# One-hot operands moved from ScalarE to VectorE, and a pacing term taken out, in a transformer block with retrieved experts

## The chip, the core and the metric

The kernel runs on one core of a Trainium2 chip. Its engines have queues of their own and meet only at semaphores: TensorE (PE: matmuls and transposes), VectorE (DVE), ScalarE (ACT), GpSimd (POOL, here only the issuer of gathers) and SyncE (SP, here only the issuer of weight loads). Everything is float32. The metric is the device time of one launch in microseconds; lower is better.

## What is computed

512 tokens of width 1024 go through two blocks. The first has three kinds of attention, one of them over compressed keys, and a gated feed-forward part. The second has a short convolution, a gated recurrence, and an expert layer. Two pieces matter here. The compressed keys are a small two-layer network over blocks of 32 tokens:

```python
blocks = kv[:, idx] + pe[None, None, :, None, :]
return jax.nn.gelu(flat @ w1) @ w2          # flat: 2048 wide, w1: 2048 x 256, w2: 256 x 64
```

And the expert layer picks, for each token and each of 8 heads, 16 of 16384 experts by a top-16 over pair sums, so 128 experts in all:

```python
expert = i1 * N_KEYS + i2                    # two indices of 0..127
u = jnp.take(u_tab, eb, axis=0)
a = gelu(einsum('td,thkd->thk', xb, u));  w = gates * a
vv = jnp.take(v_tab, eb, axis=0)
y = einsum('thk,thkd->td', w, vv)
```

## The kernel before

**Groups.** The 512 tokens are four tiles of 128 (t = 0 to 3), worked in two groups g of two tiles. Each group runs through project, attend, merge, mlp, mixer and queries. The expert layer of a group is a list of steps (`EXPERTS[g]`, written by `expert_steps`): `best`, `pairs`, `numbers` (the top-16 of one head), `job` (one gathered row per token, used by one VectorE instruction over 128 x 1024) and `spread` (below). POOL issues one gather of 512 KB per job, as early as the slot it goes to is free, which is when VectorE has done the job that used the slot before. There are 7 slots in group 0 and 12 in the first 128 jobs of group 1.

**Pacing.** The steps of group 0 are laid beside the dense work of group 1. TensorE's program decides where: `mm` adds the estimated time of each matmul to `state["spent"]`, and `take`, called for each PSUM bank, ticks off steps against it. The index reached is noted in `paced`, and VectorE and ScalarE run their steps up to that index (`catch_up`) before they touch that bank. TensorE executes no instruction for these steps, so its own order does not depend on them. At the start of attend in group 1, `settle` brings the list to a fixed step, the gate weights of tile 0, and sets `spent` to zero.

**compressed(g)** computes the hidden layer of the compression: four banks (`hid`, two for keys and two for values), each 16 matmuls, then the second layer (`kct`, `vcb`), which VectorE copies out of PSUM at L1198 and L1206. In group 1 all this stands ahead of `settle`. The first score of attend needs the copy `CQ` (L1312), which VectorE does behind the steps that `settle` demands.

**The dense tiles.** Tiles 1 and 2 (`DENSE`) don't gather their v rows. They turn their 128 weights per token into a full 128 x 128 map over the experts, and multiply that with the whole v table, read once in 128 pieces of 512 KB by SP. The map is made four tokens at a time, q = 0 to 31 for each tile: two operands of 128 x (4 x 128), `LEFT` (a one-hot of the first index, times the weight) and `RIGHT` (a one-hot of the second index), then four matmuls of 128 x 128 into one bank, and a copy of the bank into `SPREAD` by ScalarE (`keep`). For tile 1 there are two pairs of operand buffers, for tile 2 three, so the operands of q can be written when the matmuls of q - 2 (tile 1) or q - 3 (tile 2) are done.

Who makes the operands is decided by `scalar_right(t, q)`. ScalarE makes a one-hot as |iota - index| (four instructions, L2161), then 1 minus that, clipped at zero (one, L2166); LEFT is scaled by the weight (four, L2171). VectorE makes RIGHT in one instruction of 128 x 512 (L1652) and the weighted LEFT in four (L1649). Before, ScalarE makes LEFT and RIGHT of tile 1 for all q; for tile 2, VectorE makes all LEFT and the RIGHT of odd q, and ScalarE the RIGHT of even q.

**Order on VectorE in group 1.** The spread steps of tile 1 stand between the top-16 steps and jobs of tile 2: q = 0 and 1 behind head 3, groups of three behind heads 4 to 7, then two in every eight jobs. The spread steps of tile 2 follow when tile 2's weights (`aw`) are complete, four spreads to one job. On TensorE all of tile 1's spreads come first, then the transposes of tile 2's weights (L1068), then tile 2's spreads, then the multiplication with the v table, which waits for both maps.

Of the kernel before, what the change touches and what calls it, by code (L numbers as in the profile page):

```python
# [29 lines left out]
DENSE = (1, 2)  # L30
# [262 lines left out]
def build(nc, a):  # L293
    ctx = ExitStack()
    with ctx:
# [241 lines left out]

        def scalar_right(t, q):

            return t == DENSE[0] or q % 2 == 0  # L540

        def ones_before(t, q):

# [22 lines left out]
        def tensor(e, real):  # L566
            w = Waits(e, real)
            state = {"bank": 0, "tile": 0, "spent": 0.0, "side": None, "at": 0, "until": 0, "quiet": False}
# [29 lines left out]
            def take(key, *until):  # L598

                if state["side"] is None:  # L600
                    state["spent"] = 0.0
                if not state["quiet"]:
                    tick()
                pace(*key)
                while state["bank"] % 8 in held:
                    state["bank"] += 1
                b = state["bank"] % 8
                state["bank"] += 1
                for s, k in drained[b]:
                    w.wait_ge(*s[k])  # L610
                drained[b] = list(until)
                bank_of[key] = b
                return banks[b], b

            def mm(out, lhsT, rhs, start, stop):
                state["spent"] += 4 * rhs.shape[-1] / 2400.0
                return e.matmul(out, lhsT, rhs, start=start, stop=stop)  # L617

            def tile():
                i = state["tile"]  # L620
                state["tile"] += 1
                w.wait_ge(*w_in[i % RING]["w", i])
                return i, tile_view(i)

            def last_use(i, s, *key):
                done_by[i] = s, key
# [50 lines left out]
            def compressed(g):  # L677
                c0, nb = (0, 15) if g == 0 else (15 + 16 * (g - 1), 16)
                ntot = c0 + nb
                FB = FBF[g].rearrange("p (a b c) -> p a b c", a=2, b=16)[:, :, :, 0:2 * nb]  # L680
                for kv in range(2):
                    (i0, w0), (i1, w1) = tile(), tile()
                    for m in range(2):
                        pb, _ = take(("hid", g, kv, m), (a_cmp, ("hid", g, kv, m)))
                        w.wait_ge(*d_cmp["fb", g, 1])
                        for c in range(16):
                            k = mm(pb[:, 0:2 * nb], (w0, w1)[c // 8][:, c % 8, m * P:m * P + P], FB[:, kv, c, :],
                                   c == 0, c == 15)
                        state["spent"] += 5.0
                        k.then_inc(*p_cmp.mark("hid", g, kv, m))  # L690
                    last_use(i0, p_cmp, "hid", g, kv, 1)
                    last_use(i1, p_cmp, "hid", g, kv, 1)
                    yield
                w.wait_ge(*cw_in["cw", g, 1])
                for q in range(2):
                    pb, _ = take(("kct", g, q), (d_cmp, ("kct", g, q)))
                    w.wait_ge(*a_cmp["hid", g, 1, 1])
                    lo, hi = q * 31 + c0, q * 31 + ntot
                    mm(pb[0:64, 0:nb], W2[g][0][:, 0, :], HID[:, 0, 0, lo:hi], True, False)
                    mm(pb[0:64, 0:nb], W2[g][0][:, 1, :], HID[:, 0, 1, lo:hi], False, True).then_inc(  # L700
                        *p_cmp.mark("kct", g, q))
                yield
                for q in range(2):
                    pb, _ = take(("vcb", g, q), (d_cmp, ("vcb", g, q)))
                    lo, hi = q * 31, q * 31 + ntot
                    mm(pb[0:ntot, 0:64], HID[:, 1, 0, lo:hi], W2[g][1][:, 0, :], True, False)
                    mm(pb[0:ntot, 0:64], HID[:, 1, 1, lo:hi], W2[g][1][:, 1, :], False, True).then_inc(
                        *p_cmp.mark("vcb", g, q))
                yield
                w.wait_ge(*a_proj["feat", g, 12])  # L710
                for par in range(2):
                    pb, _ = take(("ce", g, par), (d_cmp, ("ce", g, par)))
                    w.wait_ge(*d_cmp["kct", g, 1])
                    for i in range(GB):
                        for hh in range(3):
                            q = (2 * hh + par) // 3
                            k = mm(pb[:, (i * 3 + hh) * 32:(i * 3 + hh) * 32 + ntot],
                                   QF[par * 64:par * 64 + 64, 5 + hh, i * P:(i + 1) * P],
                                   KCT[par * 64:par * 64 + 64, q * 31:q * 31 + ntot], True, True)
                    k.then_inc(*p_cmp.mark("ce", g, par))  # L720
                    yield
                    yield
                    yield
                    yield
                for par in range(2):
                    pb, _ = take(("pct", g, par), (a_cmp, ("pct", g, par)))
                    w.wait_ge(*d_cmp["cp", g, par])
                    for i in range(GB):
                        k = e.transpose(pb[0:96, i * P:(i + 1) * P],
                                        CE[g][:, par, 3 * i:3 * i + 3, :].rearrange("p h c -> p (h c)"), IDENT)  # L730
                    k.then_inc(*p_cmp.mark("pct", g, par))
                    for i in range(GB):
                        pb, _ = take(("oc", g, par, i), (d_cmp, ("oc", g, par, i)))
                        w.wait_ge(*a_cmp["pct", g, par])
                        w.wait_ge(*d_cmp["vcb", g, 1])
                        mm(pb[:, 0:192], PCT[g][0:96, par, i, :], VCB[0:96, par, :], True, True).then_inc(
                            *p_cmp.mark("oc", g, par, i))
                    yield
# [321 lines left out]
            def spread():  # L1060

                state["side"] = None
                for j, t in enumerate(DENSE):
                    pb, _ = take(("turned", t), (a_wts, ("turned", t)))
                    w.wait_ge(*d_exp["aw", t])
                    w.wait_ge(*d_wts["half", t])
                    for c, src in enumerate((AA[t % 2], HALF[t][:, 0, :], HALF[t][:, 1, :])):
                        k = e.transpose(pb[:, c * P:(c + 1) * P], src, IDENT)  # L1068
                    k.then_inc(*p_wts.mark("turned", t))
                    for q in range(P // 4):  # L1070
                        pb, _ = take(("spread", t, q), (a_wts, ("spread", t, q)))
                        if t == DENSE[1] or not scalar_right(t, q):
                            w.wait_ge(*d_wts["ones", t, q])
                        if t == DENSE[0] or scalar_right(t, q):
                            w.wait_ge(*a_wts["ones", t, q])
                        for i in range(4):
                            k = mm(pb[:, i * P:(i + 1) * P], RIGHT[ones_of(t, q)][:, i, :],
                                   LEFT[ones_of(t, q)][:, i, :], True, True)
                        k.then_inc(*p_wts.mark("spread", t, q))
# [33 lines left out]
        def vector(e, real):  # L1113
# [522 lines left out]
            def spread(t, q):  # L1636


                weighted = t == DENSE[1]
                if scalar_right(t, q) and not weighted:  # L1640
                    return
                w.wait_ge(*a_wts["turned", t])
                if ones_before(t, q) is not None:
                    w.wait_ge(*p_wts[ones_before(t, q)])
                left, right = LEFT[ones_of(t, q)], RIGHT[ones_of(t, q)]
                if weighted:
                    for i in range(4):
                        n = 4 * q + i
                        k = e.tensor_scalar(left[:, i, :], IOTA, TURNED[t][:, 1, n:n + 1],  # L1649
                                            TURNED[t][:, 0, n:n + 1], ALU.is_equal, ALU.mult)  # L1650
                if not scalar_right(t, q):
                    k = e.tensor_tensor(right, IOTA.unsqueeze(1).to_broadcast([P, 4, P]),  # L1652
                                        TURNED[t][:, 2, 4 * q:4 * q + 4].unsqueeze(2).to_broadcast([P, 4, P]),
                                        ALU.is_equal)
                k.then_inc(*d_wts.mark("ones", t, q))
# [679 lines left out]
```

## Time and profile before

| | us |
|---|---|
| median of 3 runs | 2629.33 (2623.28 to 2630.24) |
| the profiled execution, its own time | 2630.24 |
| its span in the profile | 2628.4 |
| PE busy / DVE busy / ACT busy / POOL busy | 2229.4 / 1593.6 / 636.4 / 943.1 |
| chain that ended last, by engine | PE 45%, DVE 25%, DMA 16%, POOL 7%, ACT 3% |
| DMA over the span | 683.54 MB, mean 260 GB/s |

In a timeline row the first number is the start in us from the start of the span, the second the time from the first start to the last end of the xN instructions merged in it. In brackets stands the idle time of the engine ahead of the row and what ended it. The page's shares are means over stages with different limits: the first third is bound by TensorE, the middle by VectorE and the gathers, the last 500 us by the DMA engines.

### The profile page before, as it was taken

How to read it: one execution, taken by the hardware profiler on the slowest of the kernel's cores; microseconds unless marked ns; L12 is line 12 of the kernel's file. 1: busy time of each engine (PE TensorE's matmuls, PEld its weight loads, DVE VectorE, ACT ScalarE, POOL GpSimd, SP SyncE). 2: the span in 40 equal slices, each digit the busy share in tenths (PEclk: the TensorE clock that was granted, in tenths of full speed). 3: DMA queues.
4: the chain of work that ended last, by engine and by line, in shares of the span. 5: the costliest groups of instructions: out<-in, count | busy, mean ns of one | idle time of the engine just before them, and what ended most of it. 6: DMA issues, size and time to landing. Idle time of an engine off the chain costs nothing.

```text
span 2628.4 us, 24800 instructions
## 1 busy us (share of the span) xinstructions
PE 2229.4 (85%) x8716; PEld 1559.5 (59%) x8716; DVE 1593.6 (61%) x3592; ACT 636.4 (24%) x1777; POOL 943.1 (36%) x772
## 2 busy tenths in 40 slices
PE   6999989998979898898899968776633489999992
PEld 6877758845848776676588626645523444444441
DVE  0022312202436778899677775876998999866667
ACT  2223212203211222332121103102699620000000
POOL 0000000000003333554346574644567446554554
PEclk9979989998989986898999988887755699999996
DMA  5432344443337787787889998977779679999997
GB/s 162 138 97 89 105 136 151 154 144 119 127 120 269 265 266 256 258 309 260 285 309 400 370 398 293 347 262 256 254 231 350 216 272 404 409 408 409 409 407 288
DMA packets 296689, 683.54 MB, mean 260 GB/s; under 512 B 21234, under 2 KB 134130, under 8 KB 296308
## 3 DMA queue, kind: packets, MB, share of 16 engines
q0 software_dynamic: 110592, 402.70, 41.6%
q1 hardware_dynamic: 179904, 266.54, 29.7%
q10 hardware_dynamic: 6068, 12.71, 1.4%
q8 instruction: 69, 1.13, 0.2%
q14 instruction: 56, 0.46, 0.0%
HBM read 679.78 MB, written 2.10 MB: 259 GB/s over the span
## 4 chain that ended last, share of the span: by engine, by line
PE 45%; DVE 25%; DMA 16%; POOL 7%; issue 4%; ACT 3%; ACTq 0%; DVEq 0%
PE bank L617 43%; DVE SLOT L1717 9%; DMA SLOT<-in_peer_v,EI 8%; POOL SLOT L2259 7%; DMA SLOT<-in_peer_u,EI 6%; DVE ACC L1731 2%; PE bank L643 1%; DVE X L1731 1%; DMA W<-in_w_up 1%; DVE H L1649 1%; DVE PB L1279 1%; ACT XS L1813 1%; ACT XS L1797 1%; PE bank L768 1%; DVE OH L1618 0%
## 5 line engine op out<-in xcount | busy, mean ns | idle before, releaser
L2259 POOL DMA_INDIRECT SLOT<-in_peer_u,EI x512 | 650.3, 1270 | 1385.8 <-DVE T L1571 816.6
L617 PE MATMUL bank<-HT,W 128*128 128x256 f32 x4032 | 936.4, 394 | 21.5 <-issue 8.3
L617 PEld LDWEIGHTS bank<-HT,W 128*128 128x128 f32 x4032 | 790.6, 198 | 147.3 <-issue 22.0
L1717 DVE CUSTOM_DVE_ANT_0 SLOT<-SLOT,H 128x1024 f32<-128x1024 f32 x384 | 454.6, 1219 | 44.3 <-DMA SLOT<-in_peer_u,EI 43.1
L2259 POOL DMA_INDIRECT SLOT<-in_peer_v,EI x256 | 292.5, 1143 | 277.2 <-DVE ACC L1731 134.1
L617 PE MATMUL bank<-H,SPREAD 128*128 128x512 f32 x680 | 304.4, 598 | 4.8 <-DMA H<-in_peer_v 4.7
L617 PEld LDWEIGHTS bank<-H,SPREAD 128*128 128x128 f32 x680 | 124.9, 190 | 178.0 <-issue 128.1
L1731 DVE SCALAR_TENSOR_TENSOR X<-SLOT,AA,X 128x1024 f32<-128x1024 f32 x128 | 164.4, 1284 | 78.9 <-DMA SLOT<-in_peer_v,EI 76.4
L1717 DVE CUSTOM_DVE_ANT_0 SLOT<-SLOT,ACC 128x1024 f32<-128x1024 f32 x128 | 153.8, 1221 | 41.2 <-DMA SLOT<-in_peer_u,EI 40.9
L1731 DVE SCALAR_TENSOR_TENSOR ACC<-SLOT,AA,ACC 128x1024 f32<-128x1024 f32 x128 | 164.1, 1282 | 19.4 <-DMA SLOT<-in_peer_v,EI 13.0
L617 PE MATMUL bank<-JK,SPREAD 128*128 128x512 f32 x344 | 157.0, 599 | 3.9 <-DMA JK<-in_peer_v 3.6
L617 PE MATMUL bank<-W,UT 128*128 128x512 f32 x352 | 151.4, 592 | 0.0
L617 PEld LDWEIGHTS bank<-JK,SPREAD 128*128 128x128 f32 x344 | 63.0, 190 | 92.9 <-issue 64.3
L617 PEld LDWEIGHTS bank<-W,UT 128*128 128x128 f32 x352 | 66.9, 190 | 83.3 <-issue 83.2
L617 PE MATMUL bank<-H 128*128 128x128 f32 x296 | 59.3, 367 | 61.0 <-ACT H L2171 53.7
L643 PE MATMUL bank<-FIX,XS 128*128 128x128 f32 x128 | 31.0, 422 | 91.0 <-ACT XS L1813 91.0
L617 PE MATMUL bank<-JK 128*128 128x128 f32 x216 | 46.6, 383 | 69.9 <-ACT JK L2171 62.1
L617 PEld LDWEIGHTS bank<-H 128*128 128x128 f32 x296 | 51.7, 265 | 68.3 <-ACT H L2171 54.6
L1797 ACT ACTIVATE XS<-X 128x1024 f32<-128x1024 f32 x20 | 21.0, 1052 | 288.7 <-DVE X L1380 148.7
L1922 ACT ACTIVATE PB<-PB,NM 128x128 f32<-128x128 f32 (+2 forms) x88 | 48.7, 553 | 161.7 <-DVE NM L1279 161.2
L617 PEld LDWEIGHTS bank<-JK 128*128 128x128 f32 x216 | 40.0, 277 | 76.3 <-ACT JK L2171 63.1
L1279 DVE CUSTOM_DVE_ANT_0 PB<-bank,BIAS 128x128 f32<-128x128 f32 (+2 forms) x72 | 34.2, 475 | 81.6 <-PE bank L617 79.6
(297 smaller groups left out, 2417.5 us busy)
## 6 DMA issues: line engine op xcount, KB each, us to landing
W<-in_w_in SPq DMA_DIRECT2D x68, 1024.0 KB, 6.2
W<-in_w_up SPq DMA_DIRECT2D x44, 1024.0 KB, 5.4
H<-in_peer_v SPq DMA_DIRECT2D x85, 512.0 KB, 6.8
JK<-in_peer_v SPq DMA_DIRECT2D x43, 512.0 KB, 6.8
W<-in_w_down SPq DMA_DIRECT2D x20, 1024.0 KB, 5.2
W<-in_peer_wq SPq DMA_DIRECT2D x16, 1024.0 KB, 5.6
W<-in_w_o SPq DMA_DIRECT2D x8, 1024.0 KB, 5.1
W<-in_w_out SPq DMA_DIRECT2D x8, 1024.0 KB, 6.6
```

The lines of the kernel that those rows point to most:

```text
L617: return e.matmul(out, lhsT, rhs, start=start, stop=stop)
L643: k = e.transpose(pb[:, c * P:(c + 1) * P], XS[t][:, (half * 4 + c) * P:(half * 4 + c + 1) * P], IDENT)
L768: k = e.transpose(pb[:, j * P:(j + 1) * P], PB[u % 3][:, j * P:(j + 1) * P], IDENT)
L1279: e.tensor_tensor_reduce(out=PB[u % 3][:, 0:wd], in0=ps("score", g, u)[:, 0:wd], in1=t, scale=-1.0, scalar=3.0e38, op0=ALU.add, op1=ALU.mi ...
L1649: k = e.tensor_scalar(left[:, i, :], IOTA, TURNED[t][:, 1, n:n + 1], TURNED[t][:, 0, n:n + 1], ALU.is_equal, ALU.mult)
L1717: e.tensor_tensor_reduce(out=x, in0=x, in1=NORMED[t], scale=1.0, scalar=0.0, op0=ALU.mult, op1=ALU.add, accum_out=AA[t % 2][:, k:k + 1]).t ...
L1731: e.scalar_tensor_tensor(SUM[t], x, AA[t % 2][:, k:k + 1], SUM[t], ALU.mult, ALU.add).then_inc(*d_exp.mark("job", t, i))
L1797: e.activation(XS[t], X[:, t, :], ACT.Square, accum_out=SS[:, t:t + 1]).then_inc(*a_norm.mark("sq", g, name, t))
L1813: e.activation(XS[t], X[:, t, :], ACT.Copy, scale=SS[:, t + 8:t + 9]).then_inc(*a_norm.mark("xs", g, name, t))
L1922: e.activation(s, s, ACT.Exp, bias=NM[:, n, il:il + 1], scale=-1.0, accum_out=LS[:, n, il:il + 1]).then_inc(*a_att.mark("exp", g, u))
L2259: e.indirect_dma_start(out=SLOT_OF[s], out_offset=None, in_=a["peer_v_2"] if i >= P else a["peer_u_2"], in_offset=bass.IndirectOffsetOnAxi ...
```

## The change

Two edits. `scalar_right` now gives ScalarE the RIGHT operand of tile 1 for even q and of tile 2 for every fourth q; VectorE makes the others, 16 more in tile 1 and 8 more in tile 2. And the hidden layer of the compression no longer adds 5 us per bank to `spent`.

```diff
         def scalar_right(t, q):
 
-            return t == DENSE[0] or q % 2 == 0
+            return q % (2 if t == DENSE[0] else 4) == 0
...
                             k = mm(pb[:, 0:2 * nb], (w0, w1)[c // 8][:, c % 8, m * P:m * P + P], FB[:, kv, c, :],
                                    c == 0, c == 15)
-                        state["spent"] += 5.0
                         k.then_inc(*p_cmp.mark("hid", g, kv, m))
```

The line that follows decides what VectorE waits for in a spread step that it now has to do (it is not in the diff, and stands in `spread` of the vector program): `w.wait_ge(*p_wts[ones_before(t, q)])`, the matmuls of q - 2 in tile 1 and q - 3 in tile 2. The orders of TensorE, POOL and SP are the same before and after; line numbers behind the second edit are lower by one.

VectorE in group 1, where the compressed keys are copied out. Before (L1717 is a job, here of tile 0, two rows each; the last steps of head 7 are already done):

```order
L1717 ISA SLOT_73,AA_88<-SLOT_73,H_80 128x1024
L1717 ISA AA_88 128x1
L1198 COPY KCT<-bank 64x16 x4
L1206 COPY VCB<-bank 31x64 x6
L1717 ISA SLOT_74,AA_88<-SLOT_74,H_80 128x1024
L1717 ISA AA_88 128x1
```

After, the same place:

```order
L1716 ISA SLOT_72,AA_88<-SLOT_72,H_80 128x1024
L1716 ISA AA_88 128x1
L1197 COPY KCT<-bank 64x16 x4
L1205 COPY VCB<-bank 31x64 x6
L1600 CAST IF<-I_204 128x32
L1601 TENSOR_TENSOR OH<-T_203 128x256
L1570 MAX CSC<-OH 128x8
L1574 MAX_INDEX CIX<-CSC,OH 128x8
```

The copies KCT and VCB now come 32 rows earlier. Behind them, and still ahead of CQ, stands what stood ahead of them before: `pairs` and `numbers` of tile 0's last head, the start of its gates (L1695), and eight jobs.

VectorE in group 1 among the top-16 steps of tile 2, behind head 5. Before:

```order
L1717 ISA SLOT_221,AA_88<-SLOT_221,H_80 128x1024
L1717 ISA AA_88 128x1
L1571 MAX T_203<-SCORED_201 128x8 x2
L1575 MAX_INDEX I_204<-T_203,SCORED_201 128x8 x2
L1579 MATCH_REPLACE SCORED_201<-T_203,SCORED_201 128x128 x2
```

After (x2: RIGHT of q = 5 and of q = 7, both into the one RIGHT buffer of tile 1's odd q):

```order
L1716 ISA SLOT_221,AA_88<-SLOT_221,H_80 128x1024
L1716 ISA AA_88 128x1
L1651 TENSOR_TENSOR H_80<-FIX,TURNED 128x512 x2
L1570 MAX T_203<-SCORED_201 128x8 x2
L1574 MAX_INDEX I_204<-T_203,SCORED_201 128x8 x2
```

One or two such instructions stand behind each of heads 3 to 7, two only behind heads 5 and 7, and then one in every eight jobs.

ScalarE in tile 1's spreads, an odd q and the even q behind it. Before:

```order
L2161 ACTIVATE H_80<-FIX,TURNED 128x128 x8
L2166 ACTIVATE H_80<-H_80 128x512 x2
L2171 ACTIVATE H_80<-H_80,TURNED 128x128 x4
L2183 COPY SPREAD_226<-bank 128x37x4
L2183 COPY SPREAD_227<-bank 128x16x4
L2183 COPY SPREAD_228<-bank 128x70x4
L2183 COPY SPREAD_229<-bank 128x5x4
L2161 ACTIVATE JK<-FIX,TURNED 128x128 x8
L2166 ACTIVATE JK<-JK 128x512 x2
L2171 ACTIVATE JK<-JK,TURNED 128x128 x4
```

After:

```order
L2160 ACTIVATE H_80<-FIX,TURNED 128x128 x4
L2165 ACTIVATE H_80<-H_80 128x512
L2170 ACTIVATE H_80<-H_80,TURNED 128x128 x4
L2182 COPY SPREAD_226<-bank 128x37x4
L2182 COPY SPREAD_227<-bank 128x16x4
L2182 COPY SPREAD_228<-bank 128x70x4
L2182 COPY SPREAD_229<-bank 128x5x4
L2160 ACTIVATE JK<-FIX,TURNED 128x128 x8
L2165 ACTIVATE JK<-JK 128x512 x2
L2170 ACTIVATE JK<-JK,TURNED 128x128 x4
```

For the odd q four of the eight L2161 and one of the two L2166 are gone.

## Rows read from the trace of the kernel before

**Rows 1.** windows; us, busy us (count) of PE, PEld, DVE, ACT, POOL; PEclk, DMA share, GB/s

```profile
1000.00:1225.00 225.00, 200.91 (x859) 144.32 (x857) 206.09 (x577) 69.69 (x179) 108.96 (x91) 0.86 0.78 266
1870.00:1959.00 89.00, 31.08 (x120) 26.72 (x120) 86.45 (x243) 84.21 (x276) 49.36 (x38) 0.51 0.68 219
1959.00:2037.00 78.00, 29.06 (x112) 24.94 (x112) 66.95 (x110) 77.03 (x256) 62.24 (x52) 0.50 0.94 342
2037.00:2068.00 31.00, 6.22 (x24) 5.34 (x24) 30.19 (x74) 15.03 (x50) 23.14 (x18) 0.50 0.89 321
2068.00:2123.00 55.00, 39.43 (x260) 35.07 (x261) 53.41 (x164) 45.23 (x113) 9.94 (x11) 0.89 0.38 118
2123.00:2350.00 227.00, 222.54 (x506) 92.41 (x505) 188.88 (x461) 3.46 (x4) 131.70 (x110) 1.00 1.00 395
```

**Rows 2.** VectorE's timeline around the copies of the compressed keys, group 1

```profile
968.79 0.17 DVE L1601 CAST IF<-I 128x32 f32<-128x32 uint32 x1
984.03 0.08 DVE L1717 DVE_READ_ACCUMULATOR2_ANT AA<- 128x1 f32 x1
995.09 0.78 DVE L1198 COPY KCT<-bank 64x16 f32<-64x16 f32 x4 [10.98 <-PE bank L617]
1001.38 0.16 DVE L1312 COPY CQ<-bank 128x8 f32<-128x8 f32 x1
```

**Rows 3.** chain of work that ended last: start us, us, what; around 1000 us

```profile
996.78 6.15 PE bank L617 x16
1002.96 0.79 DVE SLOT L1717
1003.75 0.54 DVE XS L1272
```

**Rows 4.** the same chain, in the feed-forward part of group 1

```profile
1446.23 24.22 DMA W<-in_w_up
```

**Rows 5.** ScalarE's timeline, one q of tile 1's spreads and the next

```profile
1913.01 2.46 ACT L2161 ACTIVATE JK<-FIX,TURNED 128x128 f32<-128x128 f32 x8
1915.49 1.15 ACT L2166 ACTIVATE JK<-JK 128x512 f32<-128x512 f32 x2
1918.48 2.45 ACT L2161 ACTIVATE H<-FIX,TURNED 128x128 f32<-128x128 f32 x8
```

**Rows 6.** TensorE's timeline: tile 1's last spread, then tile 2's transposes

```profile
2049.25 2.07 PE L617 MATMUL bank<-H 128*128 128x128 f32 x8 [3.40 <-ACT H L2171]
2068.43 0.47 PE L1068 MATMUL bank<-FIX,AA 128*128 128x128 f32 x1 [17.11 <-DVE AA L1723]
```

**Rows 7.** VectorE's timeline: behind heads 3, 5 and 7 of tile 2

```profile
1883.66 0.48 DVE L1571 MAX8 T<-SCORED 128x8 f32<-128x128 f32 x2
1917.19 0.48 DVE L1571 MAX8 T<-SCORED 128x8 f32<-128x128 f32 x2
1950.73 0.28 DVE L1695 TENSOR_TENSOR GW<-CSC 128x128 f32<-128x128 f32 x1
```

**Rows 8.** waits, 1959 to 2068 us: engine, tile, line, releaser; us, times, longest

```profile
DVE SLOT L1717 <- DMA SLOT<-in_peer_u,EI: 10.2, 19, 1.1
```

**Rows 9.** POOL's groups, first 1950 to 1977 us, then 1977 to 2036 us

```profile
L2259 POOL DMA_INDIRECT SLOT<-in_peer_u,EI x15 | 24.4, 1628 | 6.6 <-issue 4.0 <-DVE AA L1717 2.3 <-DVE GW L1704 0.3
L2259 POOL DMA_INDIRECT SLOT<-in_peer_u,EI x43 | 48.5, 1128 | 13.1 <-issue 13.1
```

**Rows 10.** POOL's timeline at 1948 us

```profile
1948.79 1.68 POOL L2259 DMA_INDIRECT SLOT<-in_peer_u,EI  x1 [2.33 <-DVE AA L1717]
1954.41 1.99 POOL L2259 DMA_INDIRECT SLOT<-in_peer_u,EI  x1 [0.30 <-issue]
```

**Rows 11.** VectorE's timeline in tile 2's spreads

```profile
2078.42 0.67 DVE L1652 TENSOR_TENSOR H<-FIX,TURNED 128x512 f32<-128x512 f32 x1
2079.03 1.20 DVE L1717 CUSTOM_DVE_ANT_0 SLOT<-SLOT,ACC 128x1024 f32<-128x1024 f32 x1
```

**Rows 12.** waits, 2068 to 2123 us

```profile
PE bank L617 <- DVE H L1649: 4.7, 4, 1.2
```

## The prediction

> **What bounds the kernel now.** I read three places, since the change touches three. First the table by stretches [rows 1]: in which stretch is VectorE full, in which the DMA engines? Then the chain of waits, to see whether the end hangs on that engine there. Then the timelines of the engines at the edited places, for what each waits for.
>
> From 1000 to 1225 us (attend of group 1) VectorE is busy 206.09 of 225 us, and the chain goes over to it at 1002.96, in a job and then in the first score [rows 1, 3]. Ahead of that, from 984.1 to 995.09, VectorE stands idle for 10.98 us: it has done all steps asked of it and waits for TensorE to bring the second layer of the compression [rows 2]. From 1870 to 1959 (top-16 and jobs of tile 2, tile 1's spreads beside them) VectorE is busy 86.45 of 89 us, ScalarE 84.21 [rows 1]. Both look full, and they are not equal: TensorE's last spread of tile 1 is over at 2051.3 (2049.25 + 2.07), and its next instruction then waits 17.11 us for VectorE's weights of tile 2 [rows 6]. So ScalarE's work on tile 1's map has 17 us of slack, and VectorE has none. From 1959 to 2037 VectorE waits for gathers, 10.2 us in 19 waits [rows 8], from 2037 to 2068 it is full again (30.19 of 31), and in tile 2's spreads too (53.41 of 55, ScalarE 45.23), where TensorE waits for L1649 [rows 1, 12]. Behind 2123 the DMA engines are full, share 1.00 at 395 GB/s [rows 1]: that stretch moves a fixed number of bytes and can only start earlier or later.
>
> **Part 1, the pacing term.** Nothing is added. On VectorE 32 rows change sides with the copies of the compressed keys. In the trace they begin at 968.79 and end at 984.11 (984.03 + 0.08): 15.3 us [rows 2]. Before, they lay in the shadow of the compression's matmuls. After, VectorE does two jobs, reaches KCT at 968.8 and waits until 995.09, 26.3 us instead of 11.0. The 15.3 us of steps then stand between VCB and CQ, so CQ goes from 1001.38 to 1016.7. Behind CQ on VectorE stand the decay term and the first score, behind the score ScalarE's exponential, behind that TensorE's first turn: all of attend starts 15.3 us later. Nothing can be stored up meanwhile: the 7 slots are full either way, and TensorE can run ahead only by three scores and one gate tile. VectorE stays full to 1225, so the delay is carried on. I take **+15.3 us**; the bounds are 0, if a later stage has room to take it all up, and 15.3.
>
> **Part 2, tile 1's operands.** ScalarE loses half of the 2.46 us of L2161 and half of the 1.15 of L2166 in each odd q [rows 5], 1.8 us, 28.9 us in 16 of them. I count this as nothing, for the 17.11 us of slack say that nothing waits for it. If VectorE were not late, the gain would be hidden there; without that cover it would be a gain, which is a rival below.
>
> VectorE gains 16 instructions. One takes 0.61 us start to start (2078.42 to 2079.03) [rows 11]. And each now waits for TensorE to be done with q - 2, with the jobs of tile 2, and so the gathers that need their slots, queued behind it. Place by place:
> - q = 1, 3, 5, 7, 9, behind heads 3 to 6, where VectorE is full: 5 x 0.61 = 3.1 us.
> - q = 7 follows q = 5 with nothing between, into the same buffer. TensorE can do q = 5 only when its RIGHT is there, and takes 2.07 us for it [rows 6]; with a little for the two hand-overs VectorE idles 2.2 us. The steps stand 16.8 us apart per head (1883.66 to 1917.19 is two heads, 33.5) [rows 7], against ScalarE's old pace of 5.47 us a q (1913.01 to 1918.48) [rows 5], 16.4 for three. So ScalarE waits for VectorE from q = 1 on, and its side of q = 5 is ready.
> - q = 11 and 13, the same again behind head 7 at 1950.73: 1.2 + 2.2 = 3.4 us. But from 1948.79 POOL no longer waits for slots (from 1954.41 on its idle time is 0.30 and its own) [rows 10], and the gathers set the pace of what follows. Its lead over the slots is small there. Bounds 0 and 3.4; I take 1.5.
> - q = 15 to 27, seven in the stretch in which VectorE waits 10.2 us for gathers [rows 8]: 4.3 us beside that wait, counted as 0, bounds 0 and 4.3.
> - q = 29 and 31, where VectorE is full: 1.2 us.
>
> That is 3.1 + 2.2 + 1.5 + 0 + 1.2 = **+8.0 us** until tile 2's weights are complete; bounds 6.5 and 14.2. The end of tile 1's spreads becomes late with it, to about 2070 by the old clock, but still ahead of the weights.
>
> **Part 3, tile 2's operands.** Eight more RIGHT on the engine that TensorE waits for: 8 x 0.61 = **+4.9 us** [rows 11, 12]. ScalarE's eight fewer (1.8 us each) free nothing that anything waits for: it has 10 us to spare in 55 [rows 1]. Bounds 0 and 4.9.
>
> The sum is 15.3 + 8.0 + 4.9 = 28.2 us, all of it ahead of the DMA-bound end, which moves as a block. On the profiled execution's 2630.24 that gives 2658.4; the median of the runs is 0.9 lower, so 2657.5.
>
> For the two last parts VectorE is the saturated engine by the rows. The Trainium skill, "Perfetto Trace Analysis", section "Optimizing Scalar/DVE Operations", advises the opposite direction in that state: if VectorE is saturated, give work to ScalarE. By that rule parts 2 and 3 cost time, and the trace agrees, with its 17.11 us wait for VectorE.
>
> **The rivals.**
> - *The first delay is taken up later.* For it: in the feed-forward part of group 1 the chain has a weight load of 24.22 us [rows 4], so there the DMA engines and TensorE decide in places. Against: that load starts when TensorE frees its buffer, and TensorE itself is late by then. Time: 2629.3 + 8.0 + 4.9 = 2642.
> - *Faster: ScalarE was the pace.* TensorE waits for ScalarE's L2171 in each q of tile 1 (3.40 us) [rows 6]. If tile 1's map decided when the v table can be read, 28.9 us would be saved, VectorE's additions would lie beside it, and with part 1 paid the time is 2629.3 + 15.3 - 28.9 = 2616. It decides only if tile 2's weights come before 2051; they come 17 us later.
> - *No change.* The steps moved behind the copies and the added operands all fall into waits (for gathers, for TensorE): within 8 us of before, 2629 to 2637. The full stretches of rows 1 speak against it.
> - *The gathers are slowed by the added instructions.* POOL takes 1628 ns a gather while VectorE runs jobs back to back, and 1128 when it waits in between [rows 9]. If each of the seven instructions in the gather-bound stretch holds POOL up by its 0.61 us, that adds 4.3, and the second wait of q = 13 may count in full, 1.9 more: 2664. The Trainium skill, "SBUF — State Buffer", section "SBUF: two separate sides", has such a rule: a VectorE instruction with two SBUF inputs holds the port pair shared with GpSimd for its whole length against GpSimd work that reads SBUF. By that rule the time is this rival's. The trace fits it, but jobs are not the added instruction, so it doesn't show it.
>
> **Chances.** Forecast (own range 2650 to 2661) 0.55; first delay taken up 0.22; gathers slowed 0.11; no change 0.07; faster 0.05. The range from 2638 to 2667 leaves out the two last cases and the far side of the fourth. A difference of 0.3% (8 us) is about what can be told from no change here: faster 0.05, same 0.07, slower 0.88.
>
> **What the changed kernel's profile would show.** Part 1: VectorE idle for 26 us ahead of KCT, then CQ at 1016.7. If attend's end (old 1225) is not 15 us later the first rival holds, and by where it catches up. Part 2: TensorE's waits in tile 1's spreads are for the new RIGHT, at L1651, more than for ScalarE; two idle times of about 2.2 us on VectorE behind heads 5 and 7; the wait ahead of tile 2's transposes stays, somewhat shorter than 17 us. From the first score to those transposes the distance grows by 8 us. Part 3: tile 2's spreads take 60 us instead of 55. The DMA-bound stretch behind keeps its length. The prediction is wrong if the transposes of tile 2 wait for nothing, or if VectorE has idle time behind 1016 that it didn't have before.

## The result and the profile after

The changed kernel takes 2657.27 us (median of 5 runs, 2651.49 to 2660.40) against 2629.05 for the kernel before in the same comparison: a ratio of 1.0109, 95% interval 1.0092 to 1.0128, or 24 to 34 us more. The forecast was 2657.5. The profiled execution took 2654.79, its span is 2653.0 (before 2630.24 and 2628.4).

First the same table by stretches, moved to where the same work now lies: attend; top-16 of tile 2; the rest of tile 1's spreads; tile 2's spreads; the DMA-bound stretch. Columns as in [rows 1].

```profile
1016.00:1241.00 225.00, 188.87 (x841) 138.69 (x842) 208.10 (x583) 70.91 (x183) 115.60 (x94) 0.86 0.80 273
1879.00:1976.00 97.00, 25.73 (x112) 23.49 (x112) 90.14 (x247) 66.98 (x221) 51.65 (x38) 0.59 0.63 205
1976.00:2089.00 113.00, 35.47 (x144) 31.69 (x144) 102.13 (x195) 82.66 (x278) 91.06 (x72) 0.53 0.91 323
2089.00:2149.00 60.00, 41.35 (x260) 36.83 (x261) 58.29 (x173) 33.16 (x74) 8.23 (x9) 0.86 0.33 107
2149.00:2376.00 227.00, 221.42 (x505) 93.00 (x504) 189.54 (x462) 3.31 (x4) 142.49 (x111) 1.00 1.01 396
```

VectorE is as full as before in attend (208.10 of 225 us) and in tile 2's spreads (58.29 of 60). In the heads of tile 2 it is less so, 93% against 97%; the idle times shown below are the reason. ScalarE is emptier: in tile 2's spreads 33.16 us of 60, before 45.23 of 55. The last stretch has kept its kind: DMA share 1.01 at 396 GB/s, before 1.00 at 395.

VectorE's timeline where the compressed keys are copied, beside [rows 2]:

```profile
996.30 0.78 DVE L1197 COPY KCT<-bank 64x16 f32<-64x16 f32 x4 [26.22 <-PE bank L617]
1017.83 0.16 DVE L1311 COPY CQ<-bank 128x8 f32<-128x8 f32 x1
```

The idle time grew from 10.98 to 26.22 us, and CQ went from 1001.38 to 1017.83. The chain of waits at that place (start us, us, what; compare [rows 3]) stays on VectorE for the whole of it:

```profile
995.68 1.59 PE bank L617 x12
1001.41 1.12 DVE SLOT L1716
...
1016.00 1.14 DVE SLOT L1716
```

Then VectorE's timeline behind head 5 of tile 2, RIGHT of q = 5 and of q = 7, and behind head 7, RIGHT of q = 13:

```profile
1927.14 0.68 DVE L1651 TENSOR_TENSOR H<-FIX,TURNED 128x512 f32<-128x512 f32 x1
1930.01 0.69 DVE L1651 TENSOR_TENSOR H<-FIX,TURNED 128x512 f32<-128x512 f32 x1 [2.19 <-PE bank L617]
...
1967.61 0.69 DVE L1651 TENSOR_TENSOR H<-FIX,TURNED 128x512 f32<-128x512 f32 x1 [2.17 <-PE bank L617]
```

And TensorE's timeline at the end of tile 1's spreads, beside [rows 6]:

```profile
2081.86 2.08 PE L617 MATMUL bank<-H 128*128 128x128 f32 x8 [8.94 <-DVE H L1651]
2089.56 0.47 PE L1067 MATMUL bank<-FIX,AA 128*128 128x128 f32 x1 [5.62 <-DVE AA L1722]
```

TensorE's last spread now waits for VectorE's new RIGHT and not for ScalarE, and the transposes of tile 2 come at 2089.56 instead of 2068.43. They still wait for VectorE, 5.62 us instead of 17.11: tile 1's map is later, but not so late that it decides. Two views of waits (engine, tile, line, releaser: us, times, longest), first 1976 to 2089, then 2089 to 2149 us:

```profile
PE bank L617 <- DVE H L1651: 59.1, 8, 12.7
...
DVE SLOT L1716 <- DMA SLOT<-in_peer_u,EI: 9.5, 13, 1.5
```

```profile
PE bank L617 <- DVE H L1651: 9.8, 13, 1.6
...
PE bank L617 <- DVE JK L1651: 5.7, 5, 1.6
```

In tile 2's spreads TensorE waits 18 times for the RIGHT of VectorE, 15.5 us. Before, it waited there 7 times for the weighted LEFT, L1649, 8.4 us ([rows 12] show four of them), and 11 times for RIGHT, L1652, but only 3.9 us. Seven of these, in the same view:

```profile
PE bank L617 <- DVE H L1652: 2.4, 7, 0.5
```

**Where the time lies.** The table gives the us between fixed points of the program, each from one profiled execution: KCT, CQ, the first transpose of the normalised input of the feed-forward part, of the mixer and of the queries, the step `halves` of tile 1 and of tile 2 (it follows the last head of a tile), tile 2's weights, the last RIGHT of tile 2, the end of the span. Between the two `halves` lie the heads of tile 2, between the second and the weights the stretch that waits for gathers.

| kernel | KCT to CQ | attend, merge | feed-forward | mixer | rest of tile 1 | heads | gathers | tile 2's spreads | to the end |
|---|---|---|---|---|---|---|---|---|---|
| before | 6.29 | 307.29 | 272.06 | 199.29 | 86.27 | 92.27 | 109.52 | 53.05 | 507.27 |
| after | 21.53 | 304.94 | 267.74 | 200.46 | 84.07 | 101.01 | 113.16 | 57.71 | 506.08 |
| e1 pacing | 21.55 | 304.97 | 269.47 | 198.92 | 86.31 | 92.32 | 117.91 | 53.07 | 506.15 |
| e2 operands | 6.30 | 307.28 | 267.96 | 199.88 | 85.69 | 101.06 | 111.37 | 57.74 | 507.23 |
| e3 tile 1 | 6.28 | 307.15 | 269.52 | 198.80 | 85.83 | 101.06 | 110.22 | 53.13 | 506.83 |
| e4 tile 2 | 6.29 | 307.17 | 268.72 | 199.19 | 86.23 | 92.31 | 113.00 | 57.73 | 505.91 |
| e5 no pairs | 6.29 | 307.16 | 269.63 | 198.58 | 85.91 | 98.44 | 115.09 | 53.06 | 507.35 |
| e6 late seven | 6.29 | 307.13 | 268.95 | 199.34 | 86.20 | 92.29 | 116.64 | 53.05 | 508.60 |
| e7 early seven | 6.29 | 307.17 | 267.88 | 199.57 | 84.53 | 101.04 | 119.42 | 53.13 | 507.51 |
| 9 us a bank | 1.85 | 306.03 | 273.26 | 200.71 | 74.60 | 92.35 | 117.98 | 53.05 | 506.48 |
| 12 us a bank | 1.84 | 310.56 | 272.58 | 199.69 | 72.16 | 92.30 | 115.17 | 53.06 | 505.11 |
| 20 of 32 | 6.29 | 307.20 | 270.37 | 200.86 | 86.21 | 92.39 | 116.45 | 53.48 | 507.15 |
| both | 1.85 | 306.09 | 272.99 | 201.01 | 74.64 | 92.31 | 109.57 | 53.58 | 505.85 |

Read down a column first. KCT to CQ, attend, heads and tile 2's spreads repeat within 0.2 us in kernels with the same code there: a difference of 1 us means something. Feed-forward (267.7 to 273.3) and gathers (109.5 to 119.4) scatter by 5.6 and 9.9 us, more than the 4.9 of part 3 and the 8.0 of part 2, and one pair of traces says nothing on them.

### The profile page after: what moved, and what is told of

The parts are those of the page before. It is cut to its first block, busy times and chain, and to the rows that moved or that the text cites. A ratio compares the mean times of both kernels' runs of the same rounds, so it can differ in the third digit from the quotient of the medians.

```text
span 2653.0 us, 24711 instructions
## 1 busy us (share of the span) xinstructions
PE 2217.4 (84%) x8716; PEld 1553.2 (59%) x8716; DVE 1606.7 (61%) x3616; ACT 597.6 (23%) x1657; POOL 947.8 (36%) x772
## 4 chain that ended last, share of the span: by engine, by line
PE 44%; DVE 26%; DMA 16%; POOL 6%; issue 4%; ACT 3%; ACTq 0%; DVEq 0%
PE bank L617 42%; DVE SLOT L1716 9%; DMA SLOT<-in_peer_v,EI 8%; DMA SLOT<-in_peer_u,EI 7%; POOL SLOT L2258 6%; DVE ACC L1730 2%; PE bank L643 1%; DVE X L1730 1%; DVE H L1648 1%; DMA W<-in_w_up 1%; DVE PB L1278 1%; ACT XS L1812 1%; ACT XS L1796 1%; PE bank L767 1%; DVE OH L1617 1%
## 5 line engine op out<-in xcount | busy, mean ns | idle before, releaser
L617 PE MATMUL bank<-W,HT 128*128 128x256 f32 (+3 forms) x384 | 83.0, 370 | 0.0
L643 PEld LDWEIGHTS bank<-FIX,XS 128*128 128x128 f32 x128 | 23.4, 211 | 99.7 <-issue 52.5
```

What stands on the lines that cost most here:

```text
L643: k = e.transpose(pb[:, c * P:(c + 1) * P], XS[t][:, (half * 4 + c) * P:(half * 4 + c + 1) * P], IDENT)
```

## The experiments

Below, "before" is the median of the kernel before in the same comparison: 2633.57 (33 runs) for e1 to e4, 2634.51 (31) for e5 to e7 and the kernel with 9 us, 2634.84 (29) for the rest. Single runs scatter by some 20 us, so each difference is given as the ratio's 95% interval turned into us.

**e1: the pacing term alone.** `state["spent"] += 5.0` is taken out, `scalar_right` is as before.

> Only the pacing term is taken out. Theory A (the prediction's terms): the 15.3 us of steps behind KCT are carried to the end, 2629 + 15.3 = 2644. Theory B (read from the changed kernel's trace, where the delay was 15.2 us at CQ but 8.7 us when tile 1's spreads began): the feed-forward stage takes up a third to a half, 2629 + 9 = 2638. Both: VectorE idle 26 us ahead of KCT and CQ 15 us later. What tells them apart inside the trace is the distance from CQ to VectorE's first step behind head 3 of tile 2: 882.3 us before, 874.6 in the changed kernel; A wants 882, B about 875. If the distance differs by some us also where nothing ahead was moved, it is scatter of that stage.

Measured: 2647.88, ratio 1.0047 (1.0026 to 1.0069), +7 to +18 us; the ratio itself gives +12.4, the two medians differ by 14.3. The times allow both theories. In its profile KCT to CQ grew by 15.26 us, attend gave 2.3 back, feed-forward and mixer lie inside what kernels without the edit show. The distance that was to decide, from CQ to VectorE's first step behind head 3, is 877.1 us, near theory B's 875; but in kernels in which nothing ahead of it was changed it goes from 876.5 (e7) to 882.3 (before), so it is scatter, as the text on record allowed. Theory B, taken up in feed-forward, has no support; theory A's 15.3 is 2.3 too high by the trace. Where the 2.3 went is seen in attend. TensorE's timeline of before, then of e1, at the same gate tile:

```profile
1088.85 6.11 PE L617 MATMUL bank<-HT,W 128*128 128x256 f32 x16
```

```profile
1105.23 4.82 PE L617 MATMUL bank<-HT,W 128*128 128x256 f32 x16
```

and the windows around and behind it (columns as in [rows 1]), before, then e1:

```profile
1080.00:1100.00 20.00, 17.58 (x76) 12.51 (x75) 15.47 (x53) 7.25 (x21) 9.86 (x8) 0.83 0.87 311
1100.00:1120.00 20.00, 17.82 (x78) 12.68 (x78) 18.07 (x47) 9.21 (x25) 11.01 (x9) 0.83 0.78 274
```

```profile
1096.00:1115.00 19.00, 16.58 (x78) 11.60 (x77) 16.06 (x53) 7.84 (x22) 10.47 (x9) 0.91 0.92 322
1115.00:1135.00 20.00, 17.82 (x93) 12.59 (x92) 19.69 (x57) 9.49 (x25) 12.96 (x10) 1.00 0.80 284
```

The same 16 matmuls take 4.82 instead of 6.11 us. The granted clock has two levels, 1.2 GHz (0.50) and 2.4 GHz (1.00), and a figure between them is a mean over a stretch: over these 16 matmuls alone it is 0.76, before 0.60, and over the windows shown 0.91 and then 1.00, before 0.83 twice. Laid beside before, instruction by instruction, VectorE in e1 is 16.7 us late at 1060 us of before and 13.2 late at 1117; the delay shrinks where the clocks differ. After shows the same 304.9, and the eight rows of the table with the old pacing term show 307.1 to 307.3. Why the later start goes with another granted clock was not tested.

**e2: the operands alone.** The other edit by itself.

> Only the operands are moved, in both tiles; the pacing term stays. Theory A: 8.0 + 4.9, 2642. Theory B: 12.4 + 4.7 as in the changed kernel's trace, 2646. The two parts of the change add up if e1 and e2 together give 28 us. Up to CQ nothing may differ from before; the distance from CQ to head 3 shows the scatter of the feed-forward stage with nothing moved.

Measured: 2646.37, 1.0052 (1.0035 to 1.0069), +9 to +18, which leaves room for both theories (12.9 and 17.1). Heads +8.79, tile 2's spreads +4.69, sum 13.5. With e1 (12.4 + 13.7 = 26.1) it gives the whole change within its interval: the two edits add, as closely as intervals of 5 us to either side can tell.

**e3 and e4: one tile each.** e3 has `return q % 2 == 0`, e4 `return t == DENSE[0] or q % 4 == 0`.

> Only tile 1's RIGHT of odd q goes to VectorE. Theory A: two idle times of 2.2 us ahead of q = 7 and 13, 16 instructions of 0.61, those in the gather-bound stretch hidden: 8.0 us, 2637. Theory B: the gather-bound stretch itself becomes longer, since POOL issues more slowly while VectorE is full; 12.4 us, 2641. From VectorE's step behind head 3 to tile 2's weights: 184.4 us before, A 192.4, B 196.8.

> Only tile 2: eight more RIGHT on VectorE. Both theories: VectorE sets the pace of tile 2's spreads, 8 x 0.61 = 4.9 us, 2634. Rival: ScalarE's relief is worth something there, less than 2 us in all. Tile 2's spreads then last 58 us from the weights to the last RIGHT instead of 53.1.

Measured: e3 2641.0, 1.0028 (1.0011 to 1.0045), +3 to +12; e4 2637.13, 1.0015 (0.9996 to 1.0034), -1 to +9. Each shows in its own column: heads +8.79 for e3, tile 2's spreads +4.68 for e4. Theory B of e3, 12.4 us with a longer stretch of gathers, lies just above the interval (11.9). Its profile can't decide it: the gathers take 110.22 us, but that column scatters by 10, and the distance named on record, from the step behind head 3 to tile 2's weights, is 193.9 us, between A's 192.4 and B's 196.8.

**e5: without the pairs.**

```diff
-            return t == DENSE[0] or q % 2 == 0
+            return q % 2 == 0 or t == DENSE[0] and q in (7, 13)
```

> The kernel before, with VectorE making the RIGHT of tile 1's odd q except q = 7 and 13 (those are the ones that directly follow another odd q on VectorE); tile 2 as before. Theory A (an idle time of 2.2 us at each of those two places, because the one buffer is rewritten at once): the step from the first to the second set of top-16 halves of tile 2, heads 3 to 7, takes 92.3 + 5 x 0.61 = 95.4 us instead of 101.06, and VectorE has no idle time of 2 us there; time about 2.5 us above before. Theory B (the additions cost because VectorE and GpSimd collide, and the two idle times are filled from elsewhere): the step stays above 98 us.

Measured: 2637.82, 1.0025 (1.0009 to 1.0042), +2 to +11. The heads took 98.44 us, neither 95.4 nor 101.06. Both idle times of 2.2 us are gone, and a new one stands on VectorE:

```profile
1961.83 0.29 DVE L1700 TENSOR_REDUCE GM<-GW 128x8 f32<-128x128 f32 x1 [2.97 <-issue]
```

GM needs the exponential of the gate weights from ScalarE, L2201. ScalarE's timeline of e5 shows why it comes late:

```profile
1953.95 0.77 ACT L2183 COPY SPREAD<-bank 128x148 f32<-128x148 f32 x4 [5.17 <-issue]
1954.58 2.45 ACT L2161 ACTIVATE H<-FIX,TURNED 128x128 f32<-128x128 f32 x8
...
1961.49 0.31 ACT L2201 ACTIVATE GW<-GW 128x128 f32<-128x128 f32 x1
```

ScalarE first stands 5.17 us at the copy of a bank whose matmuls wait for VectorE's RIGHT of q = 11 (it came at 1951.10), then makes all of q = 13 by itself, and only then the exponential. So 92.3 + 5 x 0.61 + 3.0 = 98.3, for 98.44 measured. The pairs cost what was said; what failed is that nothing would take their place. ScalarE, which I had left out as never waited for, is waited for once per tile, at the gates.

**e6 and e7: seven instructions late, or seven early.** The texts on record describe these two edits the wrong way round: they name as VectorE's the q that ScalarE makes. What ran:

```diff
-            return t == DENSE[0] or q % 2 == 0
+            return q % 2 == 0 or t == DENSE[0] and not 15 <= q <= 27    # e6: VectorE makes 15 to 27
+            return q % 2 == 0 or t == DENSE[0] and q > 13               # e7: VectorE makes 1 to 13
```

> The kernel before, with VectorE making the RIGHT of tile 1's odd q except q = 15 to 27, the seven that lie in the stretch in which VectorE waits for gathers; tile 2 as before. Theory A (those seven hide beside the gathers): the kernel is as slow as the one with all sixteen, about 7 to 8 us above before. Theory B (each costs its 0.61 us or more, against the gathers): 4.3 us less than with all sixteen, about 3 us above before.

> The kernel before, with VectorE making the RIGHT of tile 1's q = 15 to 31 only, nine instructions, seven of them where VectorE waits for gathers; tile 2 as before. Theory A: the step with heads 3 to 7 stays at 92.3 us, and of the nine only q = 29 and 31 can cost, 1.2 us: no difference that can be measured. Theory B (they slow the gathers): 9 x 0.61 = 5.5 us above before, in the stretch between the second set of halves and tile 2's weights.

By the prediction's terms the kernels that ran give: e6 nothing (the rival: +4.3), e7 3.1 + 2.2 + 1.5 = +6.8, up to 8.7. Measured: e6 2631.63, 0.9989 (0.9976 to 1.0002), -6 to +1; e7 2640.91, 1.0018 (0.9999 to 1.0036), 0 to +9. e6 excludes 4.3, so by the times the late seven cost nothing, and e7's heads show the full 8.77. The profile of e6 taken alone would say otherwise, 116.64 in the stretch of gathers. VectorE's waits there, e6 first, then e7, which has no edit in this stretch:

```profile
DVE SLOT L1717 <- DMA SLOT<-in_peer_u,EI: 14.8, 23, 1.3
```

```profile
DVE SLOT L1717 <- DMA SLOT<-in_peer_u,EI: 12.3, 18, 1.9
DVE CSC L1571 <- remote: 5.2, 1, 5.2
```

The kernel without the seven has the longer stretch (119.42). But the waits don't show the seven hidden either: VectorE waits 14.8 us for gathers in e6 and 10.2 in before, more and not less. POOL's issues say more. In before they are 53% of the chain of waits in this stretch, and with the 0.30 us between two of them they nearly fill it. POOL's groups from the step `halves` of tile 2 to its weights, before, then e6:

```profile
L2259 POOL DMA_INDIRECT SLOT<-in_peer_u,EI x71 | 87.9, 1238 | 24.2 <-issue 19.5 <-DVE AA L1717 2.9 <-DVE T L1583 0.3
```

```profile
L2259 POOL DMA_INDIRECT SLOT<-in_peer_u,EI x70 | 97.9, 1399 | 21.3 <-issue 19.8 <-DVE CSC L1571 0.3 <-DVE CSC L1583 0.3
```

So it is in all profiles. In the five kernels with added RIGHT in this stretch (after, e2, e3, e5, e6) POOL's issues take 91.6 to 97.9 us together, in the nine others 84.5 to 90.9. Against that, POOL waits for VectorE to free a slot (DVE AA) 0 to 1.8 us in the five, and 9.2 to 14.5 in seven of the nine others. Slower issues and shorter waits for slots about balance. Why the second goes with the first was not tested; part of it is a wait of VectorE that ends with no releaser of the program, taken up in the last section.

**e8: all of tile 2's RIGHT on ScalarE**, `return True`, the opposite end of part 3.

> The kernel before, with ScalarE making the RIGHT of tile 2 for every q, so VectorE loses 16 of them (16 x 0.61 = 9.8 us) and ScalarE gains 16 x 1.8 = 29 us on its 45.2 busy of 55. Theory A (both engines are near the pace of tile 2's spreads, VectorE first with 53.4 of 55 and ScalarE with 10 us to spare): ScalarE becomes the pace with 45.2 + 29 = 74 us, so the stretch from tile 2's weights on grows by 19 us, to about 2652 if before is at 2633. Theory B (the stretch is set by VectorE's jobs and by TensorE alone, and ScalarE's work is hidden): VectorE's 9.8 us are saved, about 2624.

Measured: 2651.40, 1.0060 (1.0040 to 1.0079), +11 to +21: theory A. TensorE's timeline shows the new pace, three q of tile 2:

```profile
2108.96 2.04 PE L617 MATMUL bank<-JK 128*128 128x128 f32 x8 [0.65 <-ACT JK L2166]
2111.27 2.05 PE L617 MATMUL bank<-H 128*128 128x128 f32 x8 [0.26 <-ACT H L2166]
2113.58 2.05 PE L617 MATMUL bank<-H 128*128 128x128 f32 x8 [0.26 <-ACT H L2166]
```

2.31 us a q, 32 of them 73.9 us, where the kernel before needs 53.

**20 of 32 on ScalarE**, `return t == DENSE[0] or q % 2 == 0 or q % 8 == 1`.

> The kernel before, with ScalarE making the RIGHT of tile 2 for 20 of 32 q (all even ones and q = 1, 9, 17, 25) instead of 16: VectorE 4 x 0.61 = 2.4 us less of 53.4, ScalarE 4 x 1.8 = 7.2 us more, 52.4. Theory A (VectorE sets the pace, in both directions): the stretch from tile 2's weights to the last RIGHT takes 50.7 instead of 53.05 us, 2.4 us off the time. Theory B (at the added q TensorE waits for ScalarE instead): unchanged or up to 2 us more.

Measured: 2632.91, 0.9982 (0.9964 to 1.0001), -9 to 0. The times leave it open; the stretch itself doesn't: 53.48 us, not the 50.7 of theory A. The waits of tile 2's spreads are for ScalarE now:

```profile
PE bank L617 <- ACT H L2166: 7.7, 9, 1.2
PE bank L617 <- ACT JK L2166: 6.2, 5, 2.6
```

So 16 of 32 is about the best of the four splits measured (8, 16, 20 and 32 on ScalarE). Part 3 is a loss because VectorE is first, but from the old split the way back gains nothing.

**The pacing term raised**, to `state["spent"] += 9.0`.

> The kernel before with 9 instead of 5 us per bank in the pacing term, the opposite of its removal: about 12 us more of VectorE's steps move ahead of the copies of the compressed keys, into the 11 us in which VectorE is idle there. Theory A (a delay of VectorE at the first score is carried to the end, in both directions): CQ 9 to 11 us earlier, VectorE's wait ahead of KCT gone, 2619 to 2624 if before is at 2629 to 2633. Theory B (an earlier start of attend is not carried, because TensorE or the DMA engines bind first): CQ earlier by as much, and the time unchanged.

Measured: 2616.53, 0.9945 (0.9926 to 0.9963), -20 to -10. The gain is at least as large as expected, the way to it is another. VectorE's timeline:

```profile
996.15 1.22 DVE L1717 CUSTOM_DVE_ANT_0 SLOT<-SLOT,H 128x1024 f32<-128x1024 f32 x1
997.29 0.72 DVE L1198 COPY KCT<-bank 64x16 f32<-64x16 f32 x4
998.04 1.06 DVE L1206 COPY VCB<-bank 31x64 f32<-31x64 f32 x6
999.14 0.17 DVE L1312 COPY CQ<-bank 128x8 f32<-128x8 f32 x1
```

The 10.98 us of idle time are filled, but CQ comes only 2.2 us earlier (1001.38 to 999.14), not 9 to 11. The rest of the gain, 11.67 us, appears 780 us later, in "rest of tile 1" (86.27 to 74.60). VectorE's jobs in that stretch, before and here:

```profile
L1717 DVE CUSTOM_DVE_ANT_0 SLOT<-SLOT,H 128x1024 f32<-128x1024 f32 x32 | 37.4, 1218 | 4.3 <-DMA SLOT<-in_peer_u,EI 4.1
```

```profile
L1717 DVE CUSTOM_DVE_ANT_0 SLOT<-SLOT,H 128x1024 f32<-128x1024 f32 x27 | 31.5, 1219 | 0.0
```

Dense work takes its share of steps by TensorE's estimated time, however far the list has come. Steps done early are therefore not missing in attend, but from the remainder, and there TensorE waits less: for `QT` (L2125) 13.2 us in before and 2.9 with 9.

**The pacing term at 12.**

> The kernel before with 12 instead of 5 us per bank in the pacing term, 3 more than the kernel with 9, which has no idle time left ahead of the copies of the compressed keys. Theory A (only steps that fill VectorE's idle time there are a gain, more of them delay the copies by as much): within 4 us of the kernel with 9. Theory B (every step pulled ahead of attend is a gain, because VectorE's work in attend and behind is less, and TensorE doesn't wait for it there): another 8 to 12 us off.

Measured: 2632.87, 0.9988 (0.9970 to 1.0007), -8 to +2. Theory A's place is right, its number is not: it expected no more than 4 us lost against the kernel with 9, and 16 are (by the two medians). VectorE's timeline:

```profile
1007.23 0.73 DVE L1198 COPY KCT<-bank 64x16 f32<-64x16 f32 x4
1007.98 1.06 DVE L1206 COPY VCB<-bank 31x64 f32<-31x64 f32 x6
1009.07 0.17 DVE L1312 COPY CQ<-bank 128x8 f32<-128x8 f32 x1
```

CQ is 9.9 us later than with 9, attend takes 4.5 more, and the remainder is only 2.4 us shorter. Why those last two don't balance I leave open.

**Both together**, 9 us a bank and 20 of 32.

> Both together: 9 us per bank in the pacing term, and ScalarE making the RIGHT of tile 2 for 20 of 32 q. Theory A: the two add, so about 2.4 us below the kernel with 9 alone, 15 to 17 us below before. Theory B: no different from the kernel with 9 alone.

Measured: 2618.16 (6 runs), 0.9929 (0.9902 to 0.9957), -26 to -11. Not to be told from the kernel with 9 alone, nor from theory A's 2.4 us less. Each is faster than both kernels of this case; the one-number change is enough for it.

## Why the prediction was right, step by step

*Part 1* (+15.3 expected). At CQ it is exact: KCT to CQ +15.24, the idle time 26.22 us for 26.3 expected. What failed is "the delay is carried on" in full: attend gave 2.3 back in after and e1 alike, so the term is 15.2 - 2.3 = 12.9 by the trace, and e1's timed +7 to +18 fits (15.3 would too). The first rival, which had this delay taken up later (2642), is excluded by e1's lower end of +7 us and by the sum. The kernel with 9 showed that my picture had a gap: a later CQ costs its delay, but steps done early pay at the remainder of the list and not at CQ. Here the two pictures agree, since the change did the same steps, only later, and left the remainder as it was (84.07 against 86.27).

*Part 2* (+8.0). Its 3.1 + 2.2 + 3.4 = 8.7 for the heads is there to the tenth, +8.74. I had taken 1.5 of the 3.4 for q = 11 and 13, because gathers would set the pace behind them; in this stretch the full price was paid. Whether the gathers' stretch gives some of it back can't be read from its 110 to 119 us, nor can the 1.2 for q = 29 and 31. The distance from the first score to tile 2's transposes, forecast to grow by 8, grew by 4.7 (from CQ, 1067.05 to 1071.73 us), as feed-forward was 4.3 us shorter and the gathers 3.6 longer, both inside their scatter. The 0 for q = 15 to 27 is right as a price, not in its reason: VectorE's waits for gathers did not shrink to make room for them, and POOL's issues became slower (e6). By the times, e3 puts the whole part at 3 to 12 us, and e6 its seven late ones at no more than 1. e5 showed the idle time as a buffer's: take the second RIGHT away and it goes. It also showed the one place in tile 1's part where ScalarE, costed at nothing, was not free.

*Part 3* (+4.9). Measured +4.66, e4 +4.68. The bottleneck is VectorE by a small margin: e8 and the split of 20 show ScalarE right behind.

*The end.* The DMA-bound block kept its length: 505.1 to 508.6 us in all thirteen rows of the table, whenever it began.

*The sum*: 12.9 + 8.7 + 4.7 = 26.3 us for the three columns, against 28.2 expected and 24 to 34 measured. One profiled pair shows 2653.0 - 2628.4 = 24.6; that the median was met within 0.3 us is luck, as the scatter of single runs shows.

*The other rivals.* Faster, with ScalarE as the pace: against it stands the wait of 5.62 us for VectorE's weights, still there with a later map. No change: excluded by the ratio. Gathers slowed: 2664 lies above every run of after (2660.40), and e6 excludes its 4.3 us as a price. Half of its story is there all the same: the second wait, of q = 13, did count in full, and POOL's issues did take longer in every profile with the added instructions. That VectorE holds POOL up is borne out for the jobs. In [rows 10] POOL takes 1.68 and 1.99 us to issue a gather under VectorE's jobs; in the timeline of the kernel with 9, while VectorE stands idle:

```profile
2026.20 0.94 POOL L2259 DMA_INDIRECT SLOT<-in_peer_u,EI  x1 [0.30 <-issue]
2027.44 0.94 POOL L2259 DMA_INDIRECT SLOT<-in_peer_u,EI  x1 [0.30 <-issue]
```

So VectorE's jobs, which read two inputs from SBUF, hold POOL's issues up. The Trainium skill, "SBUF — State Buffer", section "SBUF: two separate sides", gives this as a rule for a VectorE instruction with two SBUF inputs against GpSimd work that reads SBUF; the traces agree as far as the jobs go, and no run tests other instructions. It matters for the end of the kernel, for POOL's issues are 7% of the chain of before. What the added RIGHT do to them cost nothing in the time.

## What to carry to other kernels

When two engines share work, look for the one that a third waits for, and count on the other as well each single wait that is left on it (here the gates, once a tile). A pacing term that looks like an estimate of time can be what fills an idle engine ahead of a first dependency: read the idle time in front of the wait (10.98 us here), and size the term so that it is filled and no more: of 0, 5, 9 and 12 us a bank, 9 was the best here. And where an engine waits for gathers, look at what the gathers wait for: here it was less the DMA engines than POOL's issues, which the same VectorE slows down. Last, where stretches of unchanged code differ by 10 us between profiles, decide by many runs or by stretches that repeat, not by one pair of traces.

## What the runs showed of the hardware

**Two engines stand at once with no releaser.** In 8 of 14 profiles VectorE idles 2 to 9 us in the gathers' stretch, mostly in small steps of the top-16, and no semaphore of the program ended it. The timeline of the kernel with 9, VectorE, then ScalarE:

```profile
2029.06 0.09 DVE L1579 MATCH_VALUE_LOAD SCORED<-T,SCORED 128x8 f32 x1 [4.97 <-issue]
2033.95 0.49 DVE L1583 MAX8 T<-SCORED 128x8 f32<-128x128 f32 x2 [4.28 <-issue]
```

```profile
2031.85 1.15 ACT L2166 ACTIVATE H<-H 128x512 f32<-128x512 f32 x2 [9.42 <-remote]
```

POOL goes on issuing meanwhile. The kernel with both edits has 1.9 us of such idle time and 109.57 us in the stretch, this one 9.3 and 117.98. The cause stays open. A late supply of instructions would look like this, but of the profile's instruction queues no packet moved between 1984 and 2036 us in this kernel, and it is not in every long stretch (e6: 116.64, and none of it). All eight are among the nine kernels without added RIGHT in this stretch, where only before is free of it; the five with them have 0.7 us at most.

**A gather's issue has two prices.** In the kernel before it is 0.94 us beside an idle VectorE (40 issues), and 1.51 on average, up to 1.99, under jobs that run back to back (122 issues). An issue that starts 0.28 us into a job takes 1.74 and one that starts 0.35 into it 1.68, so both end 2.0 us behind the job's start; of those that start within 0.04 us of a job's start some take 0.94, inside the one job, and others 1.99. With the 0.30 between two issues a gather takes from 1.24 to 2.29 us, against 1.15 us a job: VectorE at full pace slows the supply of its own jobs.

**The clock gave some of a delay back.** 16 matmuls of 128x256 took 6.11 us at a mean granted clock of 0.60 and 4.82 us at 0.76, in the same code, where it began 16 us later (e1; after 4.83).
